# Moving a down-projection block into the next step and adding weights in the transfer

## The reference

```python
D_MODEL, SEQ, DEPTH, D_FF = 2048, 256, 2, 4 * 2048

def squared_relu_mlp(u, w1, w2):
    hdn = jnp.square(jax.nn.relu(jnp.einsum("bsd,df->bsf", u, w1)))
    return jnp.einsum("bsf,fd->bsd", hdn, w2)

for i in range(DEPTH):
    ...
    h = h + m
    h = h + squared_relu_mlp(rmsnorm(h, norm_mlp[i]), mlp_w1[i], mlp_w2[i])
    h = h + per_layer_embedding(h, p[i], norm_ple[i], ple_w_proj[i], ple_w_gate[i])
```

## Time and profile before

| | us |
|---|---|
| median of 3 runs | 2352.27 (2352.09 to 2355.26) |
| the profiled execution | 2357.7 |
| its span | 2355.9 |

### The profile page before, as it was taken

One profiled execution on the slowest core, in us unless ns is written; L12 is line 12 of the kernel. 1 busy time (PEld: TensorE's weight loads), 2 busy tenths in 40 slices (PEclk: granted clock), 3 DMA queues, 4 the chain that ended last, 5 costly groups with the idle time before them and its releaser, 6 DMA issues.

```text
span 2355.9 us, 29837 instructions
## 1 busy us (share of the span) xinstructions
PE 2249.0 (95%) x10152; PEld 1849.5 (79%) x10152; DVE 1724.8 (73%) x1897; ACT 1243.9 (53%) x1542; POOL 157.0 (7%) x183
## 2 busy tenths in 40 slices
PE   8999998999999999988999999989999999999888
PEld 8997787877877877867888888878778778778676
DVE  6998877687687686756766667676876877867565
ACT  5666655555545555546644444555455555555454
POOL 3887000000000000000000000000000000000000
PEclk9999999999999999999999999999999999999899
DMA  9452697756756757587777678767567577575873
GB/s 332 153 190 97 224 288 222 236 188 194 249 173 207 237 172 223 162 259 232 228 238 229 210 227 259 232 216 247 167 209 241 172 221 239 161 231 161 257 249 118
DMA packets 499525, 503.52 MB, mean 214 GB/s; under 512 B 261040, under 2 KB 299120, under 8 KB 498416
## 3 DMA queue, kind: packets, MB, share of 16 engines
q1 hardware_dynamic: 497600, 499.71, 67.4%
q10 hardware_dynamic: 1696, 1.67, 0.2%
q0 software_dynamic: 144, 1.05, 0.1%
HBM read 464.62 MB, written 37.75 MB: 213 GB/s over the span
## 4 chain that ended last, share of the span: by engine, by line
PE 57%; DMA 13%; DVE 6%; ACT 3%; issue 3%; SPq 3%; DVEq 0%; ACTq 0%
PE acc L635 9%; PE acc L636 9%; PE acc L637 9%; PE acc L612 8%; PE acc L614 8%; PE acc L613 8%; DMA pT<-staged 6%; DMA staged<-prows 5%; SPq L399 3%; PE tp L635 2%; PE tp L636 2%; PE tp L637 2%; DVE wlo L1455 2%; DVE prows L1377 1%; DMA raw<-in_mlp_w 1%
## 5 line engine op out<-in xcount | busy, mean ns | idle before, releaser
L1455 DVE TENSOR_TENSOR wlo<-pl,whi 128x1024 fp32r<-128x1024 f32 (+1 forms) x372 | 447.3, 1209 | 250.4 <-ACT whi L972 246.3
L972 ACT ACTIVATE whi<-pl 128x1024 fp32r<-128x1024 f32 (+1 forms) x372 | 386.4, 1046 | 300.4 <-PE acc L637 160.9
L1285 DVE TENSOR_TENSOR wlo<-raw,whi 128x1024 fp32r<-128x1024 f32 x248 | 297.0, 1221 | 144.9 <-ACT whi L867 142.2
L867 ACT ACTIVATE whi<-raw 128x1024 fp32r<-128x1024 f32 x248 | 257.5, 1055 | 214.0 <-PE acc L614 212.0
L972 ACT ACTIVATE whi<-raw 128x1024 fp32r<-128x1024 f32 x196 | 206.1, 1058 | 207.6 <-DVE raw L1466 138.9
L1455 DVE TENSOR_TENSOR wlo<-raw,whi 128x1024 fp32r<-128x1024 f32 x196 | 239.1, 1220 | 43.2 <-ACT whi L972 36.0
L612 PE MATMUL acc<-whi,b_hi 128*128 128x512 f32 x672 | 262.9, 391 | 4.7 <-DVE wlo L1285 4.7
L635 PE MATMUL acc<-whi,a_hi 128*128 128x512 f32 x596 | 240.3, 403 | 27.0 <-DVE wlo L1455 25.2
L635 PE MATMUL acc<-whi,b_hi 128*128 128x512 f32 x596 | 238.5, 400 | 27.8 <-DVE wlo L1455 26.1
L613 PE MATMUL acc<-wlo,b_hi 128*128 128x512 f32 x672 | 262.1, 390 | 0.0
L614 PE MATMUL acc<-whi,b_lo 128*128 128x512 f32 x672 | 261.9, 390 | 0.0
(11 more groups left out here) (219 smaller groups left out, 4071.7 us busy)
## 6 DMA issues: line engine op xcount, KB each, us to landing
pl<-in_mlp_w SPq DMA_DIRECT2D x368, 512.0 KB, 5.0
raw<-in_mlp_w SPq DMA_DIRECT2D x72, 1024.0 KB, 8.4
raw<-in_sc_w_in SPq DMA_DIRECT2D x48, 1024.0 KB, 6.5
raw<-in_cf_w_pw SPq DMA_DIRECT2D x64, 512.0 KB, 8.8
raw<-in_ple_w_gate SPq DMA_DIRECT2D x32, 1024.0 KB, 7.5
staged<-prows SPq DMA_DIRECT2D x240, 128.0 KB, 3.3
pT<-staged SPq DMA_DIRECT2D x56, 512.0 KB, 3.3
raw<-in_cf_w_pw SPq DMA_DIRECT2D x16, 1024.0 KB, 7.6
```

The source lines that it names most:

```text
L867: nc.scalar.activation(whi[:, e % SLOTS, :, :], raw[:, e // 2, 2 * (e % 2):2 * (e % 2) + 2, :], ACT.Copy).then_inc(hi_ready, 1)
L972: nc.scalar.activation(whi[:, ring(parity, i), c, :], source[:, c, :], ACT.Copy).then_inc(slot_hi, 1)
L1285: nc.vector.tensor_tensor(wlo[:, e % SLOTS, :, :], raw[:, e // 2, 2 * (e % 2):2 * (e % 2) + 2, :], whi[:, e % SLOTS, :, :].bitcast(F32), A ...
L1455: nc.vector.tensor_tensor(wlo[:, ring(parity, i), c, :], source[:, c, :], whi[:, ring(parity, i), c, :].bitcast(F32), ALU.subtract).then_i ...
```

## The change

1. Block 3 of a step's down-projection (four slots) is done in the next step, as slots `("e", 3, part)` set between the parts of products 1 and 5. So step k = 0 has 34 slots (`FIRST`), the others 38, the end four `e` parts (the first two as halves) before its sixteen `d` parts.
2. The second hidden half c1 is turned at slot 3 of the next step and its exchange runs under the `e` and first `d` slots; c0's operand is made at slot 4, c1's at slot 12 (13 in step 0, 11 in the end). The staging waits until the exchange before has landed, and the way back waits for the operand before it.
3. In the end the additions of the results stand at slots 15, 17 and 21, two turns at 15 and 19; the results of blocks 1 and 2 are split in the gate block.
4. The fast product has other signs, so that its weight sums are all additions. Products 5 and 7 keep VectorE's sums (four a step); for products 6 and 4 GpSimd issues a transfer of 1 MB that adds a block of `mlp_w1` onto field 0 of `raw`. ScalarE waits for it (`t2_ready`, `t4_ready`).
5. The order of the products is 1, 5, 7, 6, 2, 4, 3; `mix` moves behind product 6.

```diff
-STEP = (("m", 1, 0), ("m", 1, 1), ("m", 5, 0), ("d", 0, 0), ("m", 5, 1), ("d", 0, 1),
-        ("m", 6, 0), ("d", 0, 2), ("m", 6, 1), ("d", 0, 3), ("m", 7, 0), ("d", 1, 0), ("m", 7, 1), ("d", 1, 1),
-        ("m", 2, 0), ("d", 1, 2), ("m", 2, 1), ("d", 1, 3),
-        ("d", 2, 0), ("m", 4, 0), ("d", 2, 1), ("m", 3, 0), ("d", 2, 2), ("m", 4, 1), ("d", 2, 3), ("m", 3, 1),
-        ("r", 0, 0), ("r", 0, 1), ("r", 0, 2), ("r", 0, 3), ("r", 1, 0), ("r", 1, 1), ("r", 1, 2), ("r", 1, 3),
-        ("d", 3, 0), ("d", 3, 1), ("d", 3, 2), ("d", 3, 3))
+LATE = (("d", 2, 0), ("m", 2, 0), ("d", 2, 1), ("m", 2, 1), ("d", 2, 2), ("d", 2, 3),
+        ("m", 4, 0), ("r", 0, 0), ("m", 4, 1), ("r", 0, 1), ("r", 0, 2), ("r", 0, 3),
+        ("m", 3, 0), ("r", 1, 0), ("m", 3, 1), ("r", 1, 1), ("r", 1, 2), ("r", 1, 3))
+FIRST = (("m", 1, 0), ("m", 1, 1), ("m", 5, 0), ("m", 5, 1), ("d", 0, 0), ("m", 7, 0), ("d", 0, 1), ("m", 7, 1),
+         ("d", 1, 0), ("m", 6, 0), ("d", 1, 1), ("m", 6, 1), ("d", 0, 2), ("d", 0, 3), ("d", 1, 2), ("d", 1, 3)) + LATE
+STEP = (("m", 1, 0), ("e", 3, 0), ("m", 1, 1), ("e", 3, 1), ("m", 5, 0), ("e", 3, 2), ("m", 5, 1), ("e", 3, 3),
+        ("d", 0, 0), ("m", 7, 0), ("d", 0, 1), ("m", 7, 1), ("d", 0, 2), ("d", 0, 3),
+        ("d", 1, 0), ("m", 6, 0), ("d", 1, 1), ("m", 6, 1), ("d", 1, 2), ("d", 1, 3)) + LATE
+END = (("e", 3, 0, 0), ("e", 3, 0, 1), ("e", 3, 1, 0), ("e", 3, 1, 1), ("e", 3, 2, None), ("e", 3, 3, None),
+       ("d", 0, 0, None), ("d", 0, 1, None), ("d", 1, 0, None), ("d", 1, 1, None),
+       ("d", 0, 2, None), ("d", 0, 3, None), ("d", 1, 2, None), ("d", 1, 3, None),
...
+IN_PLACE_AFTER = {5: 1, 7: None}
+OUT_ADD, OUT_TURN, OUT_SPLIT = (15, 17, 21), (15, 19), 20
+HI0, HIDDEN1, HI1, HI1_FIRST, HI1_END = 4, 3, 12, 13, 11
...
+    def sums_after(self, i):
+
+        out = []
+        for n in self.sums:
+            _, of, part, _ = self.slots[n]
+            user = IN_PLACE_AFTER[of]
+            if i == max(n - 3, 0 if user is None else self.at("m", user, part)):
+                out.append(n)
+        return out
...
+            def stage_early(r):
+
+                stage_begin(r.T, r.x - 1)
+
+            def take_back(r):
+
+                sp.wait_ge(staged_ready, 64 * r.T + 64)
+                sp.wait_ge(operand_ready, 2 * (r.o - 1) + 2)
                 nc.sync.dma_start(xt, staged).then_inc(xt_ready, 16)
...
+            def product_source(t, n, i):
+
+                _, of, part, _ = t.slots[i]
+                if i in t.sums:
+                    act.wait_ge(slot_sum, len(t.sums) * n + t.sums.index(i) + 1)
+                elif of in (6, 4):
+                    act.wait_ge(t2_ready if of == 6 else t4_ready, 16 * n + 16)
                 else:
                     act.wait_ge(field_ready[FIELD[of]], 16 * n + 16)
...
-                o, x, y, needs = {5: (b11, b12, b11, 1), 6: (b11, b22, b11, 2), 7: (b12, b22, b12, 2),
-                                  4: (b11, b21, b11, 3)}[of]
+                b11, b12, b22 = (raw[:, f, 2 * part:2 * part + 2, :] for f in range(3))
+                o, more, needs = {5: (b11, b12, 1), 7: (b12, b22, 2)}[of]
                 dve.wait_ge(field_ready[needs], 16 * n + 16)
-                nc.vector.tensor_tensor(o, x, y, ALU.subtract).then_inc(slot_sum, 1)
+                nc.vector.tensor_tensor(o, o, more, ALU.add).then_inc(slot_sum, 1)
...
+            def add_block(layer, k, of, row, col, ready):
+
+                done = slots_of(k).at("m", {6: 5, 4: 6}[of], 1)
+                pool.wait_ge(slot_lo, first_slot(layer, k) + done + 1)
+                nc.gpsimd.dma_start(raw[:, 0, :, :], t_in["mlp_w1"][layer][row:row + 4 * P, col:col + NB]
+                                    .rearrange("(c r) n -> r c n", r=P), accum_op=ALU.add).then_inc(ready, 16)
+
+            for layer in range(DEPTH):
+                for k in range(STEPS):
+                    add_block(layer, k, 6, 4 * P, (k + 1) * 2 * NB + NB, t2_ready)
+                    add_block(layer, k, 4, 4 * P, (k + 1) * 2 * NB, t4_ready)
```

More of the change, by code:

```diff
@@ L411, in back @@
                 def back():
-                    stage_begin(r.T)
-                    stage_end(r.T)
+                    stage(r.T)
+                    nc.sync.dma_start(xt, staged).then_inc(xt_ready, 16)
                 return back
             def load_gate(layer):
-                unit, w = gate[layer], t_in["ple_w_gate"][layer]
-                load(unit.b + 1, w, NB, back=exchange(Result(mlp[layer][2], BLOCKS - 1)))
+                unit, w, r3 = gate[layer], t_in["ple_w_gate"][layer], Result(mlp[layer][2], BLOCKS - 1)
+                for q in range(TILES):
+                    tile(unit.b + 1, q, w[q * 4 * P:(q + 1) * 4 * P, NB:2 * NB].rearrange("(c r) n -> r c n", r=P))
+                    if q == 0:
+                        stage_early(r3)
+                    if q == 1:
+                        take_back(r3)
                 with sp.Fori(2, BLOCKS) as j:
@@ L480, in load_step @@
+            def load_step(layer, k):
+                t, then = slots_of(k), slots_of(k + 1) if isinstance(k, int) else STEP
+                c1 = Result(mlp[layer][0], 1) if t is FIRST else Result(chunk(layer, k - 1), 1)
+                c0 = Result(chunk(layer, k), 0)
+                for i in range(len(t)):
+                    free = freed(layer, k, i)
+                    if t.load[i] is not None:
+                        n = t.load[i] + 4
+                        if n < len(t.loads):
                             plain(layer, k, n, free)
-                        elif last:
-                            plain_end(layer, n - LOADS, free)
-                        else:
-                            plain(layer, k + 1, n - LOADS, free)
@@ new lines, in load_step @@
+                    fields = [f for f in (3, 2, 1, 0) if i == field_freed(t)[f]]
+                    for f in fields if then is not END else ():
+                        field(layer, k + 1, f, free if f == fields[0] else None)
+                    if i == HIDDEN1 - 1:
+                        stage_early(c1)
+                    if i == HIDDEN1 + 3:
+                        take_back(c1)
+                    if i == hidden_before(t) - 1:
+                        stage_early(c0)
+                take_back(c0)
@@ L667, in multiply_step @@
                             pe.wait_ge(mixed, n + 1)
-                    if kind == "d" and part == 0:
-                        if not (first and of < 2):
+                    if kind == "e" and begins:
+                        pe.wait_ge(down_free, 4 * n - 2)
+                    if kind == "d" and begins:
+                        if end and of in (1, 2):
+                            pe.wait_ge(up_free, 2 * n - 2 + of)
+                        elif end and of == 3:
+                            pe.wait_ge(acc_free, down.a + 1)
+                        elif not (first and of < 2):
                             pe.wait_ge(down_free, 4 * n + of - 1)
@@ L717, in multiply_mlp @@
+                    multiply_slot(layer, u, i, slot, parity, end_banks[of] if end and kind == "d" else down_banks[of % 2])
             def multiply_mlp(layer, u, ready):
@@ L1518, in run_end @@
[L1518 to L1533 removed]
+                first, end, gain = t is FIRST, t is END, ROW_PLE + layer
@@ L1535, in run_mlp @@
+                if end:
+                    turn(Result(down, 2).T, Result(down, 2).t)
             def run_mlp(layer, u, prev):
```

422 lines of the change are left out of this document (198 added, 224 removed), and 1 row of the table END.

## The result

The changed kernel takes **2292.5 us** (median of 4 runs, 2291.3 to 2293.5) against 2353.8 for the kernel before on the same chip: ratio 0.9737, 95% interval 0.972 to 0.9754. That is 61 us less; the forecast was 84 less. The time lies in the forecast's wide range (2246 to 2318), but not in the band of 2245 to 2285 in which the prediction itself put 0.62; it lies in the next one (2285 to 2315, 0.20), which was kept for rivals C and B. The profiled span is 2291.2 us, 64.7 less than before; the medians differ by 61.2, since the profiled execution of the kernel before was a long one (2357.7).

A forecast was written before the change was run, and what follows sets the result against it. TensorE's matmuls were taken as the floor, with 125.9 us of stalls winnable; less 12 (steps), 24 (k = 0) and 6 (ends), 84 us won from the median 2352.3 gives 2268 us, range 2246 to 2318.

The forecast's parts named there:

- rivals C and B: C: later loads, 2303 us; B: VectorE's work keeps GpSimd from writing, 2268 or 2310 us; C or B's upper end 0.20.
- The step's start: Opening of steps k = 1 to 6: 1.0 us lost in each of twelve instead of 6.0, 60 us won.
- walk: Slot-by-slot timing of a step's opening from profiled durations: TensorE waits 0.3 us at slot 4, 0.5 to 0.7 with drag.
- Weight sums: Four of eight sums per step leave VectorE, 63 us of its time; no gain itself, room for slots 9 to 20.
- The accumulating transfer: GpSimd's adding transfers for m6 and m4: 14 us to land, between 8.4 and 19.6, hidden in k = 1 to 6.
- The cover of 20 us: In k = 1 to 6, time from the m6 transfer's start behind slot 6 until slot 15's split wants it: 20 us.
- The double rate of the rule: For the adding transfers: adding reads two sources at half a copy's rate, so a sum would take 16.8 us.
- DMA as a whole: In the steps, two more MB raise each DMA engine's work from 61 us to 68 to 75 of 85 us.
- rival C: Loads in the steps get later, `pl` waits come through, 2 to 3 us per step: 2303 us; 0.20 together with B's upper end.
- k = 0: First step of each layer: field 1 stall some 7 us, m6's transfer 5 with the clock; 12 each, 6 us lost altogether.
- The ends: End of each MLP: 3 us lost each, against 18.9 and 16.9 before; 29.8 us won with k = 0's 6 deducted.
- The gates: Gate's first block: block 3's addition and turn late by 2 to 3 us again, as before, nothing won or lost.

The follow-up runs named there:

- experiment 2: Against the kernel after, the opening of the middle steps reordered: four e slots then four m slots, 2316.1 us; four m then four e, 2350.6 us.
- experiment 1: Against the kernel after, sums for products 6 and 4 made by VectorE again, no accumulating transfers: 2293.0 us.
- experiment 3: Against the kernel after, each accumulating transfer in steps k = 1 to 6 starts six slots later: 2420.8 us.
- experiment 5: Against the kernel after, separately: c0's operand behind slot 4, 2290.0 us; field 1 of k = 0 issued earlier, 2290.5; block 0's way back one slot earlier, 2290.9.
- experiment 4: Against the kernel after: block 2's way back before the embeddings' load, 2296.8 us; two DRAM staging buffers, 2294.8; block 3's whole exchange before the load, 2287.5.

## Why the prediction was right, and where it was off

- **The step's start**: right in mechanism and size. 0.8 us lost a step against 1.0 forecast; the wait at slot 4 is 0.37 us with 0.63 in all (walk: 0.3, with drag 0.5 to 0.7). The walk's "needed 10.1 plus the 0.5" for slot 5 has the 0.5 in it already; slot 5 was in time either way. Period 85.0 (forecast 85.3), clock 1.00. What the walk did not say is how narrow it is: with the m's in a row it loses 5.6 (experiment 2).
- **Weight sums**: right that they win nothing by themselves. That they "gave the room just used" is wrong: the steps are as long with all eight sums on VectorE (experiment 1).
- **The accumulating transfer**: 14 us taken for both. In k = 1 to 6 those for m6 landed after 13.0 to 14.8 us and those for m4 after 9.0 to 11.1. The 14 was the middle of two bounds and not a mechanism, so that it fits m6 is luck; a part of it, 2.8 us for GpSimd's pieces, was 1.28. The cover of 20 us is right, and ScalarE waited for these transfers twice in the whole kernel, once in each k = 0 (10.0 us in all). The double rate of the rule was 1.6 to 1.8 in traffic. The lower clock makes outlasting the cover dearer than the waits alone (experiment 3).
- **DMA as a whole**: 68 to 75 us of 85 forecast, 72.3 measured. The time lies where rival C was put, but C's 2 to 3 us a step didn't come: rival C's mechanism is there (ScalarE's waits for `pl` in all 86.7 us before, 101.3 after) and the ring hid it.
- **k = 0**: 10.2 and 9.6 us against 12 forecast; the stall for field 1 as described, but at slot 1 and not behind both m1 slots, since the sum is issued right after slot 0. The transfer for m6 landed after 11.2 and 10.8 us and cost 0 to 1.2 us; forecast 5. Without it the steps lost 10.2 and 8.4 where the walk had 7. So the 12 came near by two misses that partly cancel.
- **The ends**: the largest miss within the MLPs, 22.2 us lost against 6. The way back was priced by the sum before (3.3 us, 8.7 in all) and took 6.2 behind three loads. And before slots 17 and 21 stands a chain that the walk left out: addition, copy to `h`, two squares, split, in a row on two engines. By the starts of the matmuls slot 17 lost 1.4 us, slot 20 2.4 and 2.9, slot 21 3.0 and 1.4, and the lower clock 1.7 more in each end. Slot 20's part is the way back: with it earlier in layer 1 slot 20 waited no more, though the end and the gate together won nothing (experiment 5). That the others are the chain is read from the timelines; no run changed it.
- **The gates**: forecast "nothing won or lost", in fact 10 us lost. The failed step is the listing of SyncE's queue. In the kernel before, the way back of block 2 is issued and then the embeddings' load; the change swaps the two, and what a 2 MB load does to a small exchange behind it was not priced. Undoing the swap alone didn't help; the load has to stand behind block 3's exchange as well (experiment 4). The prediction's own condition, "the gate's first block loses over 5 us", is met in both layers.

Ends and gates, 16 + 10 us, are more than the whole difference between forecast and result; k = 0 and the steps gave 7 back.

## What to carry to other kernels

Where a stall comes from a row of fixed work at a stage's start, alternate long and short products there, and walk the loads' queue beside the splits; a cluster of short ones in front lost all that the move had won, one behind the long ones 24 of 61 us. Price each small exchange by what stands ahead of it on its issuing queue, loads included, and put large loads that nobody waits for behind it. An adding transfer frees the vector engine but costs 1.6 to 1.8 times the DMA time, and here it won nothing. Where VectorE is the bound it may pay; no run here shows such a case. And look at the next stage too before a repair is called won: a wait taken out of the end came back at the gate.

## What the runs showed of the hardware

- A 512 KB transfer from DRAM took 3.2 us on an empty queue and 7.5 behind a 2 MB load on the same one.
- Issuing isn't free either: four staging transfers took 3.0 us to issue on a free queue, 4.1, 5.5, 6.5, 8.8 and 9.9 with loads ahead of them.
- An adding transfer of 1 MB in 512 pieces costs GpSimd 1.28 us, lands 9.0 to 15.3 us after its issue, and takes 5.5 us of all 16 DMA engines, against 3.4 for a plain load of the same size (1.6 times; 1.8 by the queues' shares).
